# One weight matrix of a mixture-of-experts stream, loaded in four groups of rows instead of one

## What is computed

```
for e in range(32):                                        # w_gate, w_up, w_down: 1024 x 1024 float32 each
    gate = minimum(hf @ w_gate[e] + b_gate[e], 7.0)
    up   = clip(hf @ w_up[e] + b_up[e], -7.0, 7.0)
    act  = gate * sigmoid(1.702 * gate) * (up + 1.0)
    y    = y + combine[:, e:e+1] * (act @ w_down[e] + b_down[e])
```

## Time and profile before

| what | value |
|---|---|
| median of 3 runs | 1165.77 us |
| the profiled execution | 1165.64 us, its span 1163.8 us |
| granted TensorE clock over the span | 0.984 |
| TensorE matmul busy | 1119.4 us, 96% |
| VectorE, ScalarE, GpSimd busy | 32%, 22%, 1% |
| SyncE's DMA queue | 439.83 MB, 91.1% of 16 engines |
| read from HBM | 443.47 MB |
| 4 MB loads into `ring` | 72, median 20.9 us (down), 29.4 (up), 30.2 (gate) from issue to landing |

### The profile page before, as it was taken

One profiled execution on the slowest core, in us unless ns is written; L12 is line 12 of the kernel. 1 busy time (PEld: TensorE's weight loads), 2 busy tenths in 40 slices (PEclk: granted clock), 3 DMA queues, 4 the chain that ended last, 5 costly groups with the idle time before them and its releaser, 6 DMA issues.

```text
span 1163.8 us, 15022 instructions
## 1 busy us (share of the span) xinstructions
PE 1119.4 (96%) x6113; PEld 559.8 (48%) x6113; DVE 367.3 (32%) x894; ACT 257.9 (22%) x528; POOL 15.6 (1%) x20
## 2 busy tenths in 40 slices
PE   8999999999999999899989899999999998999998
PEld 8998989864343433243424243334233433443333
DVE  5477765641223122112121212121212121222213
ACT  6466554441111111011111111101110111111002
POOL 1000000000000000000000000000000000000000
PEclk9999999999999999999999999899989999999999
DMA  9855567799999999999999999999999999999995
GB/s 285 275 172 191 165 213 273 302 378 405 416 427 416 432 432 431 431 432 432 432 432 430 431 431 432 429 431 432 431 432 432 431 430 431 429 425 429 424 423 210
DMA packets 53645, 445.52 MB, mean 383 GB/s; under 512 B 3810, under 2 KB 32152, under 8 KB 36560
## 3 DMA queue, kind: packets, MB, share of 16 engines
q1 hardware_dynamic: 51530, 439.83, 91.1%
q0 software_dynamic: 1248, 4.20, 1.3%
q10 hardware_dynamic: 806, 0.59, 0.2%
HBM read 443.47 MB, written 1.13 MB: 382 GB/s over the span
## 4 chain that ended last, share of the span: by engine, by line
PE 72%; DMA 23%; DVE 2%; issue 1%; ACT 1%; ACTq 0%; SPq 0%; DVEq 0%
PE psum L1397 28%; DMA ring<-in_w_up 23%; PE psum L1429 14%; PE psum L1316 5%; PE psum L1013 4%; PE psum L1331 4%; PE psum L1014 4%; PE psum L1015 4%; PE psum L1339 2%; PE psum L1060 1%; PE psum L1153 1%; PE psum L1129 1%; ACT high L755 1%; PE psum L1324 1%; PE psum L1398 1%
## 5 line engine op out<-in xcount | busy, mean ns | idle before, releaser
L1397 PE MATMUL psum<-ring,xT 128*64 128x512 f32 x960 | 437.0, 612 | 35.4 <-DMA ring<-in_w_up 35.2
L1398 PE MATMUL psum<-ring,xT 128*64 128x512 f32 x960 | 437.2, 612 | 0.0
L1397 PEld LDWEIGHTS psum<-ring,xT 128*64 128x64 f32 x960 | 132.5, 141 | 313.1 <-issue 286.6
L1429 PE MATMUL psum<-ring,guT 128*64 128x512 f32 x984 | 224.5, 598 | 0.4 <-DVE guT L1903 0.4
L1884 DVE COPY gu<-psum 128x512 f32<-128x512 f32 x32 | 33.5, 1048 | 573.8 <-PE psum L1398 573.8
L1398 PEld LDWEIGHTS psum<-ring,xT 128*64 128x64 f32 x960 | 132.5, 141 | 0.0
L1429 PEld LDWEIGHTS psum<-ring,guT 128*64 128x64 f32 x984 | 65.2, 136 | 134.1 <-issue 111.4
L951 ACT COPY gu<-psum 128x512 f32<-128x512 f32 x32 | 34.0, 1061 | 420.1 <-PE psum L1398 420.1
L1574 DVE TENSOR_TENSOR low<-raw,high 128x2048 fp32r<-128x2048 f32 x31 | 71.3, 2302 | 36.5 <-ACT high L755 36.5
L1013 PE MATMUL psum<-hT_hi,high 128*128 128x256 f32 x272 | 78.3, 288 | 0.1
L1014 PE MATMUL psum<-hT_lo,high 128*128 128x256 f32 x272 | 76.9, 283 | 0.0
(11 more groups left out here) (216 smaller groups left out, 1033.6 us busy)
## 6 DMA issues: line engine op xcount, KB each, us to landing
ring<-in_w_down SPq DMA_DIRECT2D x25, 4096.0 KB, 20.9
ring<-in_w_up SPq DMA_DIRECT2D x24, 4096.0 KB, 29.4
ring<-in_w_gate SPq DMA_DIRECT2D x23, 4096.0 KB, 30.2
ring<-in_w_gate SPq DMA_DIRECT2D x12, 2048.0 KB, 19.7
ring<-in_w_up SPq DMA_DIRECT2D x12, 2048.0 KB, 17.3
raw<-in_w_in SPq DMA_DIRECT2D x22, 1024.0 KB, 5.2
ring<-in_w_down SPq DMA_DIRECT2D x7, 2048.0 KB, 12.7
ring<-in_w_down SPq DMA_DIRECT2D x11, 1024.0 KB, 29.4
```

The lines of the kernel that those rows point to most:

```text
L1397: mm(every(bank(GU + nb)[0:CAP, :]), x_k, of_chunks(gate[:, k, :], nb), start=k == 0, stop=k == KC - 1)
L1398: done = mm(every(bank(GU + nb)[CAP:P, :]), x_k, of_chunks(up[:, k, :], nb), start=k == 0, stop=k == KC - 1)
L1429: done = mm(o[half * CAP:(half + 1) * CAP, :], values[:, k, :], chunk_k[:, half * BANK:(half + 1) * BANK], start=k == 0, stop=k == KC - 1)
```

## The change

Expert 20's down matrix is loaded by four DMAs in place of one: rows (partitions) 0 to 5, 6 to 11, 12 to 15 and 16 to 127, issued one behind the other by SyncE after the same wait. Each adds 16 to the same semaphore, so `in_place` counts 4 for this matrix. Nothing else changes: the same bytes go to the same partitions, and TensorE waits for all four.

```diff
+BY_ROWS, ROWS = 3 * 20 + 2, (0, 6, 12, 16, P)
...
         def in_place(m):
-            return sum(SPLITS[k] if k < len(SPLITS) else not by_parts(k) for k in range(m % RING, m + 1, RING))
+            return sum(SPLITS[k] if k < len(SPLITS) else len(ROWS) - 1 if k == BY_ROWS else not by_parts(k)
+                       for k in range(m % RING, m + 1, RING))
...
                 for m in range(3 * RING, TAIL):
-                    if not by_parts(m):
+                    if m == BY_ROWS:
+                        free(m, 1)
+                        e, kind = MATRICES[m]
+                        for r0, r1 in zip(ROWS, ROWS[1:]):
+                            sp.dma_start(ring[m % RING][r0:r1, :, :].rearrange("p c n -> p (c n)"),
+                                         weights_of[kind][e][r0:r1, :, :].rearrange("p c n -> p (c n)")
+                                         ).then_inc(place_in[m % RING], 16)
+                    elif not by_parts(m):
                         free(m, 1)
                         load(m, 0, KC, place_in[m % RING])
```

## The result

After the change the kernel takes 1182.5 us, the median of 4 runs (1180.8 to 1184.1), against 1165.6 before (4 runs beside them): the ratio is 1.0147, 95% interval 1.0135 to 1.0159, so +17.0 us (+15.7 to +18.5). Forecast were +9.5 us and a range up to 1181.0: the sign was right, the size was not. The profiled execution took 1180.76 us.

A forecast was written before the change was run, and what follows sets the result against it. The weight stream was taken as the bound, TensorE close behind. For engines 0 to 3, 15.0 + 8.5 + 1.2 - 9.7 = 15.0 us, less the lead of 5.5, gave +9.5: 1165.8 to 1175.3 us; range 1164.2 to 1181.

The forecast's parts named there:

- The bound: Expert phase: the weight stream at 431 GB/s sets the pace, so a delay of it reaches the end in full.
- who carries the rows: Changed loads: 6 rows run on 6 engines, 4 on 4, 112 on 16; engines 0 to 3 carry 10 rows.
- rival A: Changed loads: every row at full pace, so the loads balance the engines, 1164.6 to 1165.8 us; chance 0.28 together with D.
- B: Changed loads: full pace, but engines 0 to 3 are of the late half, 2 rows more, 1168.2 us; chance 0.05.
- D: Changed loads: rows are cut over all engines at full pace, no change; counted with rival A, chance 0.28.
- Rival C: Small loads hold up all 16 engines, lead absent, or 112 rows collide: 1180 to 1181 us, both up to 1186; chance 0.09.
- the 112 rows at +1.2 us: Load of rows 16 to 127: one row of an engine's seven at a bit over half pace, 1.2 us; upper bound 5.7.
- the lead of 5.5 us as a cover: At 826 us the early half of the engines leads by about 5.5 us, taken off the delay of engines 0 to 3.
- 15.0 us for three narrow rows: Loads of 6, 6 and 4 rows: engines 0 to 3 each take three rows at 5.0 us instead of 1.22.
- The forecast at full pace, -1.2 us: Changed loads at full pace: ten engines save one row, 1.22 us, and the lead covers 2.4 us more on engines 0 to 3.
- The wait at matrix 64: TensorE's wait for expert 21's up matrix: near 14 us instead of 4.45, with landing near 855 instead of 845.7.
- theory P: From the experiments' expectations: neighbouring partitions share a receiving path; a load whose rows reach few paths at a time is slow.

The follow-up runs named there:

- e13: Kernel before, with expert 20's down matrix as one load of 64 rows, source rows 0 to 63 into partitions 32 to 95, other half left out: 1160.13 us.
- e14: Kernel before, with expert 20's down matrix as one load of 64 rows, source rows 32 to 95 into partitions 0 to 63: 1169.51 us.
- e1: The changed kernel with expert 20's down matrix as two loads, 16 rows and 112 rows: 1180.86 us, +15.6 on the kernel before.
- e11: Kernel before, with only rows 32 to 95 of expert 20's down matrix loaded, to the same partitions: 1159.87 us, -5.3.
- e12: Kernel before, with only rows 0 to 63 of expert 20's down matrix loaded, to the same partitions: 1170.01 us, +4.9.
- e3: The changed kernel with expert 20's down matrix as two loads of 64 rows: 1179.99 us, +14.7 on the kernel before.
- e10: Two loads of 64 rows for expert 5's down matrix instead of expert 20's: 1175.75 us, +10.2 on the kernel before.
- e15: The change itself moved from expert 20's to expert 5's down matrix: 1180.0 us, +15.3 on the kernel before.
- e16: The changed kernel's four loads cut by chunks instead of rows, each 128 rows of 8 KB: 1164.52 us, -0.1 on the kernel before.
- e5: The changed kernel with loads of 6, 6, 4, 6, 2 and 104 rows, small loads into partitions 4 apart: 1185.54 us, +20.0 on the kernel before.
- e6: The changed kernel with loads of 6, 6, 4, 6, 2 and 104 rows, all into neighbouring partitions: 1191.24 us, +25.7 on the kernel before.

## Why the prediction was right in sign and wrong in size

*The bound, right.* The stream sets the pace, and a delay at 806 us is still there at the end: 16.7 us at matrix 64, 16.6 at the last wait, and in the time of the same execution 15.1, because of the lower clock that the one before had at its end. Right too were the price of the issues (1.32 us for four, nothing on the path), who carries the rows (51,546 packets in SyncE's queue against 51,530: the 16 more are 6 + 6 + 4 + 16 completions less 16), and that the receiving side has the limit (e13, e14, for loads of 64 rows). Nor did the small loads land together with the 112 rows, which would have been rival A's sign: by the semaphore's records the engines complete the three small ones between 814.6 and 826.5 us and the 112 rows between 830.9 and 843.3. Rival A needed full pace for the small loads, B too; D needed no change. All three fell with the rate of 170 to 249 GB/s. Rival C named both mistakes, and its 1180 to 1181 for either of them was nearest, with a chance of only 0.09; both together would have been 1185 to 1186.

*The step that failed first: the 112 rows at +1.2 us.* They were priced as nearly a full load because they cover 112 partitions. e1 has them at half pace: 7 rows at 210/16 = 13.1 GB/s for an engine are 17.5 us, 9.0 more than 8.5. They are the larger part of the cost. The upper bound was wrong too: 5.7 took 351 GB/s as the full pace, that of the early `raw` stage, and not the 431 of the stream in which the load stands. With 431/210 it would have been 8.9, and the range would have held the result. Nor was breadth the right measure: 64 partitions run at full pace or at half, by which ones they are (e11, e12), and 112 run at half.

*The step that failed second: the lead of 5.5 us as a cover.* The sum treats each engine as a clock of its own, so that an early engine may be late for free. The lead itself was there (5.4 us from the first to the last engine at matrix 62, before). But the engines aren't apart: while some are in a slow load, the others are slow as well (DMA share 1, half the rate, for 30 us; no row under 2.34 us from 815 to 820 and under 2.39 from 820 to 825; e3 against e10). The trace of before had it in small: where `down_bias` passes, the 16 KB rows of the weights that start between 250.8 and 252.6 us took 0.80 us or more, against a median of 0.61 in the 5 us ahead. That matrix 61 came late shows it most plainly. It was issued before the change's loads; the first engine completed it at 811.0 us, the last at 821.5, so its last rows, on the late engines, ran beside early engines that were already in them.

*The third term: 15.0 us for three narrow rows.* With the first two mended, the sums are these. All take 17.5 for the 112 rows, or 20.0 for 128 rows at half pace, less 9.7; the foreign traffic at expert 20 is e3's 3.5.

| kernel | sum | measured |
|---|---|---|
| e10, 64 and 64 rows, expert 5 | 20.0 - 9.7 = 10.3 | 10.2 |
| e3, 64 and 64 rows, expert 20 | 10.3 + 3.5 = 13.8 | 14.7 |
| e1, 16 and 112 rows | 5.0 + 17.5 - 9.7 + 3.5 = 16.3 | 15.6 |
| e15, the change at expert 5 | n + 17.5 - 9.7 = 7.8 + n | 15.3, so n = 7.5 |
| the change | n + 17.5 - 9.7 + 3.5 = 11.3 + n | 17.0, so n = 5.7 |

With 5.0 for one narrow row the sum fits e1, though no row there took over 3.8 us. Three of them leave 5.7 to 7.5, not 15. This n is what is left of the sum, not a time that was measured. By the packets, rows of 5.0 to 5.3 us did occur in e15, but with the change at expert 20 none took over 4.4; and in e15 half of the rows that start between 385 and 395 us took 2.1 us or less, not the 2.5 that 17.5 us for seven rows supposes. Why the sum by loads overstates the whole isn't shown further; the profile doesn't number the engines. The price had a weak base as well: of the 60 rows of `onehot` and the mask 51 start in the window of 351 GB/s and only 9 in the one of 210 from which the 5.0 was worked out. The table also warns of a coincidence: the old sum with only the 112 rows mended, 15.0 + 17.5 - 9.7 - 5.5 = 17.3, hits the change exactly. It says 22.8 for e15, where no lead is to be had and 15.3 were measured.

*The balance.* The forecast at full pace, -1.2 us, stays untested. The last engine ended 0.8 us nearer to the mean, but in e16, which balances nothing, it ended 1.3 us nearer.

*The wait at matrix 64* was to be 14 us and is 9.91, while the landing was to be 855 and is 862. Both come from the same cause: TensorE had waited 8.1 us earlier, for matrices 61 and 62, so it came later itself. A delay has to be read from the landing; the wait is only what is left of it. The granted clock also fell to 0.66 where TensorE had idled (820 to 825 us), against 1.00 in that window before, but TensorE waits again afterwards, so this costs nothing of its own.

*Open:* why 112 rows in partitions 16 to 127 run at half pace, though they reach nearly all partitions, and so whether theory P is the whole rule. Which engine gets which rows would tell, and the profile doesn't show it.

## What to carry to other kernels

Keep the loads of a stream like this one, which fills the engines at 431 GB/s, at 128 partitions, and split them along the free dimension if they must be split: four loads of 128 rows cost nothing (e16), four loads of the same bytes by rows cost 17 us. Before you price a load by its bytes or its number of partitions, ask which partitions it reaches, and take the whole stream at the slow rate for as long as any engine is in it; a lead of some engines is an addition then. To see whether a slow load holds up its neighbours, divide the engines' busy time in a short window by the rows in it. Take both bounds of an unseen cost from the full rate of the stage where it will stand.

## What the hardware showed

A load of 64 partitions runs at full rate or at half, by its place: 32 to 95 landed in 14.2 and 14.4 us, 0 to 63 in 24.4 and 26.3. One slow load of 2 to 4 MB halved the rate of all 16 engines (210 GB/s at a DMA share of 1.0), with an earlier matrix of the same queue among what was slowed: a row of 32 KB took 2.4 to 2.8 us on every engine in e3 (815 to 835 us) in place of 1.21 to 1.23. 112 of 128 rows ran no faster than 64 (203 to 216 GB/s). And early in the stream the loads of 6, 6 and 4 neighbouring rows pulled the whole stream to 118 to 144 GB/s for 10 us (e15). A load of 104 rows ran on 13 engines (e5, e6).
